# Zero fill moved to later places, the expert loop peeled, and the last two experts' results distributed by TensorE

## The reference, cut to what matters

```python
def hierarchical_moe(h, w_rg, b_rg, w_re, b_re, w_gu, w_dn):
    ...                                  # top-1 of 4 groups, then top-2 of 4 experts in it
    comb = jnp.sum(jax.nn.one_hot(expert_idx, N_EXPERTS, dtype=f32) * (top_p * p_grp)[..., None], axis=1).astype(x.dtype)
    y = jnp.zeros_like(x)
    for e in range(N_EXPERTS):
        a, u = jnp.split(x @ w_gu[e], 2, axis=-1)
        y = y + comb[:, e:e + 1] * ((jax.nn.silu(a) * u) @ w_dn[e])
    return y.reshape(B, S, D)

xs = xs + g2 * hierarchical_moe(h, *moe_w)
y_sample = rmsnorm(xs, final_norm)       # y_prompt likewise from the context tokens
```

## Time and profile before

| what | us |
|---|---|
| three runs | 728.24, 735.43, 737.33 |
| median | 735.43 |
| profiled execution, its own time | 727.59 |
| its span in the profile | 725.8 |
| mean granted PE clock in it | 0.956 of 2.4 GHz |

### The profile page before, as it was taken

How to read it: one execution, slowest core, us unless ns; L and a number is a source line. 1 busy time by engine, 2 the same in 40 slices (tenths; PEclk the granted TensorE clock), 3 DMA queues, 4 the chain that set the end, 5 groups by cost and what they waited for, 6 DMA issues and landing times.

```text
span 725.8 us, 7482 instructions
## 1 busy us (share of the span) xinstructions
PE 648.3 (89%) x2596; PEld 357.0 (49%) x2596; DVE 358.2 (49%) x715; ACT 160.6 (22%) x414; POOL 95.5 (13%) x120
## 2 busy tenths in 40 slices
PE   3799999999949999999999899995999999999910
PEld 3343574345525555567777744442744444444400
DVE  3325453421425665347555626857444455554337
ACT  6000200002022221226656713222100101010013
POOL 1042100131100301020322310111100000000040
PEclk9999999999969999999999999998799999999965
DMA  8999815804964288999300249415799999999266
GB/s 290 386 272 329 323 54 184 311 1 146 381 241 146 109 355 297 421 358 420 141 1 13 105 170 389 195 65 198 299 320 362 369 339 370 361 365 395 86 231 260
DMA packets 63908, 182.48 MB, mean 251 GB/s; under 512 B 5655, under 2 KB 19343, under 8 KB 59781
## 3 DMA queue, kind: packets, MB, share of 16 engines
q1 hardware_dynamic: 54088, 157.53, 59.4%
q0 software_dynamic: 4384, 12.48, 5.0%
q10 hardware_dynamic: 5404, 12.06, 4.3%
HBM read 122.71 MB, written 59.30 MB: 251 GB/s over the span
## 4 chain that ended last, share of the span: by engine, by line
PE 82%; DVE 6%; DMA 5%; issue 2%; ACTq 2%; SPq 1%; ACT 1%; POOL 1%; DVEq 0%; POOLq 0%
PE PS L1559 23%; PE PS L1938 15%; PE PS L1954 8%; PE PS L1792 7%; PE PS L1551 5%; PE PS L1707 5%; PE PS L1779 2%; PE PS L1590 2%; DMA PR<-in_w_ada 2%; ACTq L782 2%; DMA PR<-scratch_mod 1%; PE PS L1686 1%; PE PS L1922 1%; PE PS L1736 1%; PE PS L1500 1%
## 5 line engine op out<-in xcount | busy, mean ns | idle before, releaser
L1559 PE MATMUL PS<-RING,hT 128*128 128x512 f32 x400 | 182.2, 604 | 0.8 <-DVE hT L1019 0.8
L1559 PEld LDWEIGHTS PS<-RING,hT 128*128 128x128 f32 x400 | 74.3, 193 | 87.5 <-issue 86.8
L1938 PE MATMUL PS<-PR,RING 128*128 128x512 f32 x192 | 86.8, 602 | 1.2 <-DVEq L1392 1.2
L1792 PE MATMUL PS<-RING,hT 128*128 128x512 f32 x160 | 72.7, 600 | 0.0
L1938 PEld LDWEIGHTS PS<-PR,RING 128*128 128x128 f32 x192 | 36.4, 193 | 44.1 <-issue 44.1
L1792 PEld LDWEIGHTS PS<-RING,hT 128*128 128x128 f32 x160 | 29.0, 190 | 30.5 <-issue 30.5
L1954 PE MATMUL PS<-PR,TMP 128*128 128x512 f32 x96 | 43.2, 592 | 0.0
L1707 PE MATMUL PS<-RING,hT 128*128 128x256 f32 x160 | 36.9, 384 | 0.7 <-ACT TMP L850 0.6
L1551 PE MATMUL PS<-hT,RING 128*128 128x512 f32 (+3 forms) x128 | 37.1, 449 | 0.0
L940 ACT ACTIVATE TMP<-PS 128x256 f32<-128x256 f32 x16 | 6.2, 385 | 131.5 <-PE PS L1938 131.5
L996 DVE TENSOR_TENSOR TMP<-PS,TMP 2x512 f32<-2x512 f32 x24 | 16.4, 682 | 36.6 <-PE PS L1590 32.1
(11 more groups left out here) (327 smaller groups left out, 912.9 us busy)
## 6 DMA issues: line engine op xcount, KB each, us to landing
scratch_xs<-fnorm SPq DMA_DIRECT2D x16, 2560.0 KB, 20.8
PR<-in_w_gate_up SPq DMA_DIRECT2D x12, 2048.0 KB, 19.1
PR<-in_w_ada SPq DMA_DIRECT2D x20, 1024.0 KB, 10.2
RING<-in_w_in SPq DMA_DIRECT2D x14, 1024.0 KB, 7.4
PR<-in_w_down SPq DMA_DIRECT2D x12, 1024.0 KB, 21.6
hT<-in_w_gate_up SPq DMA_DIRECT2D x4, 2048.0 KB, 18.2
scratch_xs<-RING ACTq DMA_DIRECT2D x16, 512.0 KB, 10.2
RING<-scratch_xs SPq DMA_DIRECT2D x56, 128.0 KB, 12.1
```

What stands on the lines that cost most here:

```text
L1559: last = mm(PS[:, bank, :], hTv[:, k, t * P:(t + 1) * P], ring[:, ci % 2, k, :], start=(k == 0), stop=(k == KD - 1))
L1792: last = mm(PS[:, i % 4, :], hTv[:, k, t * P:(t + 1) * P], ring[:, (WOUT + q) % 2, k, :], start=(k == 0), stop=(k == KD - 1))
L1938: last = mm(PS[:, 4 + b, :], xgT[:, b, k, :], gub[s][:, k, :], start=(k == 0), stop=(k == KD - 1))
```

## The change

1. **Fill.** The fill after scan step g=3 is gone; experts 0 to 2 are filled after g=7, 3 to 7 after g=9, and 8 to 15 (before: 12 to 15) ahead of the last projection chunk.
2. **Entry.** The ranks of the last tile are computed ahead of the transposes; the first expert's rows are transposed and completed first; the second expert's last-tile matmuls stand inside the first expert's gate and up. The first two pairs stand ahead of PE's loop, which runs over quads 1 and 2; the last quad is written out behind it. PE reads the loop bound between the second and third pair.
3. **End.** The results of the last two experts (14 and 15) aren't stored. POOL waits only for the stores of the last quad's first pair, and gathers while the last pair is computed. DVE builds for every tile and both late experts a weighted one-hot matrix (`late_hot`: the weight where the token's rank is the row's number), PE transposes the ten matrices, ACT copies them out, and PE multiplies them with `yo` (`late_rows`, 20 matmuls of 128x512). The weights `early` are zero for a token whose expert is 14 or 15. DVE adds the gathered rows inside the last pair (`early_sum`), and the PSUM sums behind it (`late_sum_in`).

The diff, cut:

```diff
-    ZERO_AFTER = {3: (0, 1, 2, 3), 7: (4, 5, 6), 9: (7, 8, 9, 10, 11)}
+    ZERO_AFTER = {7: (0, 1, 2), 9: (3, 4, 5, 6, 7)}
...
-                for e in range(12, NE):
+                for e in range(8, NE):
...
-        n_rounds = pool.value_load(rnd[0:1, 0:1], min_val=1, max_val=ROUNDS)
+        end = pool.value_load(rnd[0:1, 1:2], min_val=QUADS - 1, max_val=ROUNDS * QUADS - 1)
         for b in range(2):
-            pool.wait_ge(yo_stored[b], n_rounds * (2 * QUADS * 16) + 16)
+            pool.wait_ge(yo_stored[b], end * 32 + 32)
...
+        def silu(qd, s2, b):
+
+            act.wait_ge(gu_done[2 * s2 + b], qd + 2)
+            nc.scalar.activation(sil[:, b, :], PS[:, 4 + b, 0:EH], ACT.Silu).then_inc(sil_ready, 1)
+
+        def store(qd, s2):
+
             row = (qd % QUADS) * (4 * T - 32) + qd * 32
+            for b in range(2):
+                act.wait_ge(yo_ready, qd * 4 + (2 * s2 + b + 3))
+                act.dma_start(scratch["xs"][bass.ds(row + (2 * s2 + b) * T, P), :], yo[:, b, :]).then_inc(yo_stored[b], 16)
+
+        def late_out(i):
+
+            act.wait_ge(first_done, 5 + i)
+            n_ = min(4, 2 * NT - 4 * i)
+            nc.scalar.activation(PR[:, 10240 + 4 * P * i:10240 + 4 * P * i + n_ * P], PS[:, 7, 0:n_ * P], ACT.Copy
+                                 ).then_inc(xrow_copied, 1)
...
+        silu(end, 0, 0)
+        silu(end, 0, 1)
+        late_out(0)
+        store(end, 0)
+        silu(end, 1, 0)
+        late_out(1)
+        silu(end, 1, 1)
+        late_out(2)
...
+        V.tensor_scalar(late_row, misc[:, NE - 2:NE], float(T), None, ALU.mult)
+        step(V.tensor_scalar(rt[:, 9, 0, 0:1], cnt[:, 1:2], float(P), None, ALU.mult))
+        step(V.tensor_scalar(late_row, late_row, rt[:, 9, 0, 0:1], None, ALU.add))
+        ranks_ = PS[:, 7, 0:NE * NT].rearrange("p (t e) -> p t e", e=NE)[:, :, NE - 2:NE]
+        V.tensor_tensor(late_rank, ranks_, late_row.unsqueeze(1).broadcast_to([P, NT, 2]), ALU.subtract)
+        for j in range(2):
+            last = V.tensor_tensor(late_tmp[:, j], r16[:, j, :, NE - 2:NE], cw[:, j].unsqueeze(2).broadcast_to([P, NT, 2]), ALU.mult)
+        step(last)
+        V.tensor_tensor(late_w, late_tmp[:, 0], late_tmp[:, 1], ALU.add)
+        step(V.tensor_scalar(late_in_, late_rank, 0.0, None, ALU.is_ge))
+        for j in range(2):
+            last = V.tensor_tensor(late_tmp[:, j], r16[:, j, :, NE - 2:NE], late_in_, ALU.mult)
+        step(last)
+        step(V.tensor_reduce(late_sum, late_tmp, AX.X, ALU.add))
+        step(V.tensor_tensor(late_sum, late_sum, cw, ALU.mult))
+        step(V.tensor_tensor(early, cw, late_sum, ALU.subtract))
...
+        def early_sum(t):
+
+            dve.wait_ge(pick_in[t], 32)
+            step(V.scalar_tensor_tensor(x1[:, t], ypick[t][0], early[:, 0, t:t + 1], x1[:, t], ALU.mult, ALU.add))
+            step(V.scalar_tensor_tensor(x1[:, t], ypick[t][1], early[:, 1, t:t + 1], x1[:, t], ALU.mult, ALU.add))
+
+        def late_sum_in(t):
+
+            dve.wait_ge(first_done, 8 + t)
+            for q in range(2):
+                part = x1[:, t, q * 512:(q + 1) * 512]
+                last = V.tensor_tensor(part, part, PS[:, LATE_BANK[t] + q, :], ALU.add)
+            last.then_inc(y_sum, 1)
+
+        def finish(t):
+
+            dve.wait_ge(fin_rstd, t + 1)
+            V.scalar_tensor_tensor(ypick[t][0], x1[:, t], stat[:, 16 + t:17 + t], fnorm[:], ALU.mult, ALU.mult
+                                   ).then_inc(fin_ready, 1)
...
+        gates_of(end, 0)
+        for t in range(NT):
+            for e in range(2):
+                last = V.tensor_scalar(late_hot[:, t, e], misc[:, 64:64 + P], late_rank[:, t, e:e + 1], late_w[:, t, e:e + 1],
+                                       ALU.is_equal, ALU.mult)
+        last.then_inc(onehot_ready, 1)
+        hidden(end, 0)
+        next_rows(end, 0)
+        gated_out(end, 0)
+        gates_of(end, 1)
+        hidden(end, 1, (0,))
+        early_sum(0)
+        hidden(end, 1, (1,))
+        early_sum(1)
+        gated_out(end, 1, (0,))
+        early_sum(2)
+        gated_out(end, 1, (1,))
+        early_sum(3)
+        late_sum_in(0)
+        early_sum(4)
+        late_sum_in(1)
+        finish(0)
+        for t in range(2, NT):
+            late_sum_in(t)
+            finish(t - 1)
+        finish(NT - 1)
...
+        first_rows_T(0)
+        last_tile_rows(0)
+        first_rows_T(1)
...
+        def late_transposes(i):
+
+            pe.wait_ge(onehot_ready, 3)
+            if i >= 1:
+                pe.wait_ge(xrow_copied, 2 + i)
+            for n_ in range(4 * i, min(4 * i + 4, 2 * NT)):
+                last = tr(PS[:, 7, (n_ % 4) * P:(n_ % 4 + 1) * P], late_hot[:, n_ // 2, n_ % 2], ident[:])
+            last.then_inc(first_done, 1)
+
+        def late_rows(t, e):
+
+            if t == NT - 1 and e == 0:
+                pe.wait_ge(y_sum, 1)
+            for q in range(2):
+                last = mm(PS[:, LATE_BANK[t] + q, :], late_T[:, t, e], yo[:, e, q * 512:(q + 1) * 512],
+                          start=(e == 0), stop=(e == 1))
+            if e == 1:
+                last.then_inc(first_done, 1)
...
+        def expert_pair(qd, s2, first=False, final=False):
+
+            for b in range(2):
+                s = 2 * s2 + b
+                pe.wait_ge(xgT_ready, qd * 4 + (2 * s2 + b + 1))
+                pe.wait_ge(wg_in[s], qd * 16 + 16)
+                pe.wait_ge(hid_ready, qd * 4 + (2 * s2 + b + 1))
+                for k in range(KD):
+                    last = mm(PS[:, 4 + b, :], xgT[:, b, k, :], gub[s][:, k, :], start=(k == 0), stop=(k == KD - 1))
+                    if first and b == 0 and k == 3:
+                        last_tile_rows(1)
...
+                if final:
+                    late_transposes(1 + b)
...
+        expert_pair(0, 0, first=True)
+        expert_pair(0, 1)
+        pe.wait_ge(rounds_ready, 1)
+        end = pe.value_load(rnd[0:1, 1:2], min_val=QUADS - 1, max_val=ROUNDS * QUADS - 1)
+        with pe.Fori(1, end) as qd:
             for s2 in range(2):
...
+                expert_pair(qd, s2)
+        expert_pair(end, 0)
+        late_transposes(0)
+        expert_pair(end, 1, final=True)
+        pe.wait_ge(hidT_ready, end * 4 + 6)
+        pe.wait_ge(xrow_copied, 5)
+        pe.wait_ge(yo_ready, end * 4 + 5)
+        late_rows(0, 0)
+        late_rows(1, 0)
+        pe.wait_ge(yo_ready, end * 4 + 6)
+        late_rows(0, 1)
+        late_rows(1, 1)
+        for t in range(2, NT):
+            for e in range(2):
+                late_rows(t, e)
```

More of the change, by code:

```diff
@@ L925, in _ @@
         for b in range(2):
[L926 removed]
+            act.wait_ge(first_done, 2 * b + 1)
             for k2 in range(2):
@@ L1914, in _, with last_tile_rows @@
             last.then_inc(first_done, 1)
-        ranks(NT - 1)
-        pe.wait_ge(x1T_ready, 2 * NT)
-        for b in range(2):
+        def last_tile_rows(b):
             pe.wait_ge(onehot_ready, b + 1)
-            if b == 1:
+            if b == 0:
+                pe.wait_ge(x1T_ready, 2 * NT)
+            else:
                 pe.wait_ge(xrow_copied, 1)
```

118 lines of the change are left out of this document (50 added, 68 removed).

## The result

| | before | after |
|---|---|---|
| median of the runs | 732.87 us (4 runs, 728.24 to 737.33) | 714.52 us (703.51, 713.66, 715.39, 718.90) |
| ratio | | 0.968, 95% interval [0.960, 0.975] |
| profiled execution: time, span | 727.59, 725.8 us | 715.39, 713.6 us |
| granted clock, mean | 0.956 | 0.979 |

The four runs of before are the three of the table ahead and one of 730.30. Ratios with an interval leave out slow runs (over 1.5% above the fastest of their kernel, here 715.39 and 718.90), so they are not the quotient of the medians, which is 0.975 here.

A forecast was written before the change was run, and what follows sets the result against it. PE was taken to bound the kernel (82% of the span), with gains only where it stands still. 727.59 - 10.3 - 2.3 + 0.5 - 8.5 = 707.0, plus 5 us of scatter: 712, range 701 to 722.

The forecast's parts named there:

- The fill: Mixer: without the four fills new_m's issue on ACT ends earlier and PE restarts sooner; -10.3 us (-8.1 to -13.5).
- the cold restart: Mixer, PE's transposes and eight records after the idle stretch: warm they save 2.15 us, of which 1.0 was taken.
- Rival 1: Mixer: the fill isn't what blocks new_m, so the stall stays and the rest holds; 722.3 us, chance 0.10.
- The rule that I set against the gain: Mixer: packets under 512 B are slow by themselves, so new_n's stall stays; by it alone the fill term is 0.
- The fills elsewhere: Eight fills ahead of the last ring load end around 375, 20 us ahead of that load; costed at nothing.
- The entry: Start of the experts: PE's waits of 0.61 and 1.20 us go (-1.8), plus 0.5 of clock; -2.3 us (-0.5 to -3.7).
- the register load: PE's register load and branch, now between pairs two and three; +0.5 us (0 to 1.2).
- half-clock records: Entry, first 24 gate/up records: denser work may spare some at half clock; 1.9 us at most, 0.5 taken.
- The end: Last pair: gathers from 676.2 put sums of gathered rows under it, PE not held up; -8.5 us (-5 to -10).
- Rival 4: Last pair: first gather late, DVE waits ahead of the second hidden part, PE waits for it; 748 us, chance 0.03.
- 5 us of scatter: Whole kernel: 5 of the 7.84 us between profiled execution and median of three, added to 707.0 to give 712.
- Rival 3: End: DVE becomes the bound, its chain some 6 us longer; 718 us, chance 0.10.

The follow-up runs named there:

- three fills: Kernel before with three zero fills after scan step g=3 instead of four, the fourth after slice 7: 725.65 us in one run.
- six fills: Kernel before with six zero fills after scan step g=3 instead of four: 738.14 us in one run.
- the first profile: The profiled execution among the first four runs of the full change against the kernel before: 715.39 us.
- the 702.13 us execution: The unaltered change run again, eight runs beside the kernel before: median 712.64 us, ratio 0.974; the profiled one took 702.13.
- kernels with the sums moved: Changed kernel with three early sums behind both gated outputs: 709.96 us; also with earlier row loads: 709.94; early_sum(0) behind hidden parts, early_sum(1) between gated outputs: 709.42.

## Why the prediction was right

**The fill: right in place, too small.** -10.3 forecast, 13.1 measured, inside the bound of 13.5. Two sizes: I freed ACT at 197.5 of a range 195.4 to 198.7; it was 197.12 in a program that starts 1.48 us later, 195.6, so 1.9 us more. And of the 2.15 us of the cold restart I took 1.0; all went. Rival 1 (722.3 us) did not come, and its ground was a misreading: the prediction takes most of ACT's packets for the single values of new_n, but those of the earlier trace rows are new_C's, of 512 bytes, and only the 1207 of the earlier trace rows, with 0.08 MB, are mostly single values. The rule that I set against the gain, 512 B as the least size at full rate (the Trainium skill, "DMA: Bandwidth & Descriptors", Specifications), therefore had no hold on this stall. The trace doesn't contradict it: 1175 packets that went in one us (three fills, 204 to 205) moved only 0.07 MB. There are merely few such bytes: beside no fill new_n and new_m are issued in 0.59 and 1.57 us. That ACT is blocked for as long as the fill lasts is what the six fills corrected: with four both readings give the same time.

**The fills elsewhere cost nothing:** right. SP's issue, not the transfer, grew to 36 us, and 39 us of cover remained.

**The entry: too small.** -1.8 with its +0.5 forecast, 4.6 measured by shift and 4.75 by medians. Of the waits that I took away, 1.81 us went and 0.56 came back ahead of the first gate/up, behind the addition on DVE; the register load cost nothing instead of 0.5. What I mis-sized was the clock: "I take 0.5" of the 1.9 us of half-clock records. It gave 1.5 (12.23 against 3.70 and 7.03), and 0.65 more in the transposes, which I had not counted. The rest of the 4.6, about 1 us, I have not taken apart.

**The end: the step that failed** is "the queue is empty about 675.3 ... gathers from 676.2 ... So PE isn't held up". In the first profile, where PE is 16.2 us earlier than before, they should have started at 660.0 and started at 670.74. In the 702.13 us execution, 17.4 us earlier, they should have started at 658.8 and started at 660.04, and there the end gave 8.9 us, against 8.5 forecast. I read the empty queue in one execution of before, in a stretch where nothing of that kernel was urgent, and moved it with PE's time as if it were a property of the loop, while the DMA engines had been full up to it. Rows that I had pointed the other way: stores landing after up to 15.0 us, and a loop that needs 399 GB/s where the row that I used showed 402; the windows of the loop itself, 354 and 365, I had not set against it.

**Rival 4** named the mechanism to the line: DVE waits ahead of the second hidden part, PE waits for that, from a landing after 682.3 in the old time (666.1 now; it was 677.27). I gave it 0.03 and 748 us, since I had the clock stay at half for all that was left. It came back within about 6 us of work, so the half clock cost 3.0 us and not 24. The rival's place is right, its price a third (12.6 of 36.4 us). By the times it is the usual case and not the rare one: of the twelve runs of the change nine took 711 us or more; how late the gathers were is traced in two of them only.

**Why 712 was met all the same:** by luck. The sum came to 707.0, and 5 us of scatter were added for no cause that I could name. By the measured terms it is 727.59 - 13.1 - 4.6 - 8.9 = 701 on time and about 714 late. The gains that I had too small (5.6 us) and the end that I had too good (8.5 gained, 3.7 lost) offset each other in part, and the 5 us did the rest. Rival 3, DVE as the bound, is seen only in kernels with the sums moved.

## What to carry over

When work moves from behind a loop into its last turn, its transfers meet the loop's queue: compare the bytes of a turn with the rate that the engines show *before* reading an empty queue as room, and ask whether one execution is enough to say so. Put nothing that waits for a gather ahead of something that the bounding engine wants, in any in-order queue. And a bulk transfer should not run while an engine whose sequencer also does compute issues transfers of many packets that are small beside those of the bulk.

## What the runs showed of the hardware

- Two queues with work share the engines packet for packet (345 to 345, 1.35 MB against under 0.01, with six fills; 90 to 91 from 206 to 207 in the kernel before): a queue of 4-byte or 512-byte packets beside one of 4-KB packets moves some 90 of them in a us; alone, up to 1175 small ones in one us (three fills, 204 to 205).
- An issue behind a backlog blocks the issuing sequencer: four row loads took SP 15.40 us, eight took ACT 16.71, against 0.35 each.
- The same program got 350 and 379 GB/s in the same stretch of two executions, at a share of 1.04 and 1.03, and took 715.39 and 702.13 us.
- After 8.50 us of idleness PE's granted clock was 0.50 in the next 5 us and 1.00 again some 6 us after work had resumed (0.85 from 685 to 690, 1.00 from 690 on).
